# Extra matmuls of a constant tile ahead of each sub-layer's matmuls in a two-layer decoder trunk

## The reference

```python
x = x + 0.5 * rmsnorm(swiglu(rmsnorm(x, ng[0]), ffn1_in, ffn1_out), ng[1])
x = x + rmsnorm(mixer(rmsnorm(x, ng[2])), ng[3])
x = x + 0.5 * rmsnorm(swiglu(rmsnorm(x, ng[4]), ffn2_in, ffn2_out), ng[5])
```

## Time and profile before

| what | value |
|---|---|
| median of 3 runs | 2587.87 us (2587.82 to 2588.37) |
| span of the profiled execution | 2587.0 us |
| PE busy | 2483.4 us, 12094 records |
| DVE busy | 1368.0 us |
| ACT busy | 1032.3 us |
| POOL busy | 380.9 us |
| granted TensorE clock, mean | 0.982 |

### The profile page before, as it was taken

One profiled execution on the slowest core, in us unless ns is written; L12 is line 12 of the kernel. 1 busy time (PEld: TensorE's weight loads), 2 busy tenths in 40 slices (PEclk: granted clock), 3 DMA queues, 4 the chain that ended last, 5 costly groups with the idle time before them and its releaser, 6 DMA issues.

```text
span 2587.0 us, 34928 instructions
## 1 busy us (share of the span) xinstructions
PE 2483.4 (96%) x12094; PEld 2049.8 (79%) x12094; DVE 1368.0 (53%) x1874; ACT 1032.3 (40%) x1389; POOL 380.9 (15%) x276
## 2 busy tenths in 40 slices
PE   8999998998999999999999889999999889999997
PEld 7888876887788888788888678888888777788885
DVE  5445347665454443554433667666666642644533
ACT  5333335554443233433333445454455442432332
POOL 2111011000211110111101510000000001211100
PEclk9999999998999999999999989999999999999999
DMA  5332331221232233232233111111111102222232
GB/s 164 97 97 77 96 104 58 72 73 57 65 98 97 97 84 90 86 106 97 89 88 100 67 66 50 50 35 58 50 50 58 33 26 97 73 97 97 83 96 65
DMA packets 66912, 203.32 MB, mean 79 GB/s; under 512 B 7664, under 2 KB 11888, under 8 KB 66816
## 3 DMA queue, kind: packets, MB, share of 16 engines
q1 hardware_dynamic: 66816, 202.03, 24.7%
HBM read 199.87 MB, written 2.13 MB: 78 GB/s over the span
## 4 chain that ended last, share of the span: by engine, by line
PE 86%; DVE 6%; ACT 4%; issue 4%; DMA 0%; DVEq 0%; SPq 0%; ACTq 0%
PE bank L1282 68%; PE bank L1494 6%; PE bank L1487 5%; PE bank L1547 1%; ACT w_hi L448 1%; DVE resid L768 1%; PE bank L1576 1%; DVE gate L953 1%; DVE y L763 1%; DVE h_lo L753 1%; PE bank L1567 1%; PE bank L1586 1%; DVE neg_at L1029 0%; PE bank L1429 0%; DVE w_lo L749 0%
## 5 line engine op out<-in xcount | busy, mean ns | idle before, releaser
L749 DVE TENSOR_TENSOR w_lo<-raw,w_hi 128x1024 fp32r<-128x1024 f32 x405 | 581.8, 1454 | 490.6 <-ACT w_hi L448 490.6
L1282 PE MATMUL bank<-h_hi,w_hi 128*128 128x512 f32 x1784 | 712.1, 399 | 59.7 <-DVE h_lo L753 31.9
L1282 PE MATMUL bank<-h_hi,w_lo 128*128 128x512 f32 x1784 | 701.9, 393 | 0.0
L1282 PE MATMUL bank<-h_lo,w_hi 128*128 128x512 f32 x1720 | 676.7, 393 | 0.0
L448 ACT ACTIVATE w_hi<-raw 128x1024 fp32r<-128x1024 f32 x405 | 427.1, 1057 | 581.5 <-PE bank L1282 541.3
L1282 PEld LDWEIGHTS bank<-h_hi,w_hi 128*128 128x128 f32 x1784 | 339.9, 191 | 141.5 <-issue 40.2
L1282 PEld LDWEIGHTS bank<-h_hi,w_lo 128*128 128x128 f32 x1784 | 339.5, 190 | 72.5
L1282 PEld LDWEIGHTS bank<-h_lo,w_hi 128*128 128x128 f32 x1720 | 327.4, 190 | 69.7 <-issue 3.1
L1191 POOL TENSOR_TENSOR y<-y,up 128x512 f32<-128x512 f32 x88 | 174.2, 1979 | 743.1 <-DVE up L792 670.8
L1282 PE MATMUL bank<-act_hi,w_hi 128*128 128x512 f32 x704 | 278.1, 395 | 0.0
L1282 PE MATMUL bank<-act_hi,w_lo 128*128 128x512 f32 x704 | 278.1, 395 | 0.0
(11 more groups left out here) (238 smaller groups left out, 2822.4 us busy)
## 6 DMA issues: line engine op xcount, KB each, us to landing
raw<-in_ffn_in SPq DMA_DIRECT2D x172, 512.0 KB, 3.5
raw<-in_gd_in SPq DMA_DIRECT2D x49, 512.0 KB, 3.5
raw<-in_ffn_out SPq DMA_DIRECT2D x64, 384.0 KB, 3.1
raw<-in_ffn_out SPq DMA_DIRECT2D x64, 320.0 KB, 2.9
raw<-in_hg_in SPq DMA_DIRECT2D x32, 512.0 KB, 3.5
raw<-in_gd_out SPq DMA_DIRECT2D x16, 512.0 KB, 3.7
raw<-in_hg_out SPq DMA_DIRECT2D x8, 512.0 KB, 3.5
g_bc<-g_rows SPq DMA_DIRECT2D x8, 512.0 KB, 4.4
```

The source lines that it names most:

```text
L749: nc.vector.tensor_tensor(w_lo[:, r, :], raw[:, r, :], w_hi[:, r, :].bitcast(f32), ALU.subtract).then_inc(lo_split, 1)
L1282: ins = nc.tensor.matmul(dst, w, moving[ml][:, k, :], start=first and n == 0 and (wl, ml) == (0, 0), stop=last and n == len(ks) - 1 and wl ...
```

## The change

Ahead of everything else in head_start(s), PE issues 24 matmuls (sub-layer 0) or 19 matmuls (sub-layers 1 to 5) of ones x ones, 128 x 128 by 128 columns, plain fp32, into the first 128 columns of bank 7. Nobody reads the result. In sub-layer 0 PE first waits until ones is made; in the others there is no wait ahead of them. The wait for the weight units and for h_lo of the first chunk come behind them. In all 24 + 5 x 19 = 119 matmuls are added; nothing is removed.

```diff
+WARM = 19
+WARM_FIRST = 24
...
             def head_start(s):
 
                 u0 = first_unit[s]
+                if not s:
+                    pe.wait_ge(const_made, 1)
+                for _ in range(WARM if s else WARM_FIRST):
+                    nc.tensor.matmul(bank[7][:, 0:P], ones[:], ones[:], start=True, stop=True)
                 if s:
                     pe.wait_ge(lo_split, u0 + RING + SKEW)
                 for k in range(KD):
```

## The result

| | before | after |
|---|---|---|
| median, 6 runs each | 2588.41 us (2587.82 to 2589.22) | 2596.51 us (2595.87 to 2599.37) |
| span of the profiled execution | 2587.0 us | 2597.4 us |

The changed kernel is slower: ratio 1.0034, 95% interval 1.0023 to 1.0044; the medians lie 8.1 us apart. Forecast were 2584.8 us and a range of 2582.0 to 2588.0. The profiled execution of after is its slowest one, 2599.37, so the traces differ by 10.4 us where the medians differ by 8.1.

A forecast was written before the change was run, and what follows sets the result against it. PE was taken to bound the kernel, with 86% of the chain, though DVE paces the heads from chunk 5. Gains of 1.2 + 0.3 + 1.6 = 3.1 us off 2587.87 gave 2584.8, range 2582.0 to 2588.0.

The forecast's parts named there:

- cost nothing: Heads of sub-layers 1 to 5: 4.48 us of added matmuls lie wholly under ACT's and DVE's work, 0.3 us left.
- No DMA queue is touched: Whole change: the added matmuls affect no DMA queue, since SP waits for splits and not for PE; no cost booked.
- Sub-layer 0: Its head starts 1.4 us later, at 9.1, but runs at full speed: gain 1.2 us (0.9 to 1.8).
- DVE doesn't hold it: Sub-layer 0's head: h_lo of chunk 4 is there at 19.01, PE comes to it at 20.0, so no wait.
- Sub-layers 1 to 4: Heads: DVE sets the pace from chunk 5 on, so gains are only 0, 0.03, 0 and 0.3 us.
- Rival 1: Heads: every slow matmul saved is time saved, 13.1 us, for 2574.8; chance 0.05.
- the rule of the Trainium skill: Heads: advice against idle gaps between matmul bursts; by it the change is worth half of all six slow stretches.
- rival 2: Heads: the added matmuls don't hold or raise the clock; +6.7 us in all, 2594.6; chance 0.04.
- rival 3: Heads of sub-layers 1 to 5: clock unhelped but cost hidden; time within 1 us of 2587; chance 0.06.
- Sub-layer 5: Its head has a slow stretch of 4.80 us, like sub-layer 2's 4.97, so a gain of about 0.
- Later restarts: Slow stretches from 627 and 1496, drawn anew by the earlier start: gain 1.6 us, ends -1.0 and +3.5.
- The two mixers' time shifts by more than 4 us: Sign over the two mixers, named in advance as showing the prediction wrong; size over 4 us.

The follow-up runs named there:

- shift by 144: The kernel before plus 288 satisfied waits (144 instructions) in PE's idleness ahead of the DeltaNet loop, no matmul added; 2596.53 us, ratio 1.0034.
- shift by 130: The kernel before plus 260 satisfied waits (130 instructions) ahead of the DeltaNet loop; 2590.44 us in one run.
- experiments 1 to 6: Kernels made from before or after with satisfied waits or fewer added matmuls, moving the DeltaNet loop's start or end in the code; 2586.52 to 2598.18 us.
- experiment 2: The changed kernel plus 224 satisfied waits (112 instructions) ahead of the DeltaNet loop, two blocks of shift in all; 2587.84 us, ratio 1.0001.
- experiment 5: The changed kernel plus 108 instructions of satisfied waits inside the DeltaNet loop's body, moving its end but not its start; 2596.63 us in one run.
- experiment 6: The changed kernel with 16 instead of 24 added matmuls in sub-layer 0; 2586.52 us, ratio 0.9994.
- experiment 7: The changed kernel with 18 matmuls in sub-layer 0 and more such fillers in further PE idle times of HGRN2's last step and the DeltaNet; 2581.07 us, ratio 0.9971.
- shift by 160: The kernel before plus 320 satisfied waits (160 instructions) ahead of the DeltaNet loop; 2590.72 us in one run.
- experiment 4: For the 2587.87 us quoted: the changed kernel without its 24 matmuls in sub-layer 0, those of sub-layers 1 to 5 kept; ratio 1.0.

## Why the prediction was wrong

**What failed.** The section on the parts of the change counts 4.48 us of PE time under cover and finds that the added matmuls "cost nothing" in sub-layers 1 to 5. As time of PE that is right. What it never counts is that the 119 matmuls are also 476 instructions in PE's program, and that everything behind them moves. It has no term and no rival for that, and its sentence "No DMA queue is touched" is wrong: the queue that brings PE its instructions is one, with 65 loads instead of 61. So the harm was put at nothing, where it measured 8.1 us. The mechanism as the runs leave it: at each back edge of the DeltaNet loop the code is loaded anew, first the block that holds the loop's start and then, 3.0 to 3.1 us later (up to 3.6 in some kernels without a pause), the next. The wait for the first is always there, 4.2 to 5.1 us on the branch, and always covered by the 17 matmuls in PE's queue. With enough instructions between the start and the end of its block, PE is busy with them until the second load has come. After starts the loop two instructions ahead of the end of a block, and PE waits for the second load. The traces agree in all eight pauses of four kernels (after, the shifts by 144 and 130, the longer body): PE goes on 1.2 to 1.6 us behind the end of the second load (after: 1733.94 + 1.57 = 1735.51, and 1737.07; shift by 144: 1734.33 + 1.01 = 1735.34, and 1736.55; shift by 130: 1733.44 + 0.96 = 1734.40, and 1735.63). The pauses then lower the clock. At the first edge of after start to start is 4.73 instead of 0.33, and 14 matmuls at 0.42 instead of 0.23 add 2.7: 7.1 in all, the jump that the traces show. At the second it is 4.7.

How PE takes its code, why 1.2 to 1.6 us remain behind a load, and why the second load comes 3 us behind the first, no record shows. That the place of the loop's start decides is shown, by experiments 1 to 6. That the next load is what PE waits for rests on the times above, on the pauses at one and the same instruction at 130 and 144, and on the number of loads.

**Sub-layer 0: 1.2, measured 0.2.** The added matmuls ended near 8.6 and not at 9.1, within the bounds given. The step that failed is "DVE doesn't hold it": it checked one chunk against the old times of DVE. That chunk's h_lo came at 20.67 instead of 19.01, and the one before it was late too. PE is idle for 0.75 us by that, 1.1 from start to start. This place also differs from run to run. In nine profiled kernels without a filler at the start the sum stands between 28.8 and 30.9, mean 29.8, and in five with one between 28.4 and 29.9, mean 29.4. That is 0.4 us, which a spread of 1.5 to 2.1 us doesn't tell from nothing, and 16 of them (29.4) do no worse than 24.

**Sub-layers 1 to 4: right.** In sub-layers 1, 2, 3 and 4 gains of 0, 0.03, 0 and 0.3 were forecast, and 0.04, 0.05, 0 and 0.32 measured. The largest one, PE at the end of sub-layer 4's head in after, where before has 1463.37 and the kernel was 0.46 ahead by then:

```profile
1462.59 1.02 PE L1274 MATMUL bank<-acc,ones 128*128 128x512 f32 x2
```

PE meets DVE's chain earlier and waits for it. Rival 1, all slow matmuls saved, is out by this: the clock is 1.00 at the heads and the time isn't there. (It is this rival that the prediction's paragraph on the rule of the Trainium skill means, and not the second.) So are rivals 2 and 3, since the clock does hold.

**Sub-layer 5: 0, measured 0.6 lost.** PE waits 0.97 us twice there; one addition on DVE (L770, at 2224.41) took 1.81 us instead of 0.69. It isn't the change: in the five other kernels with the same 19 matmuls there (experiments 2, 5, 6, 7 and the one without the first 24) the distance to before stays the same over this head within 0.02 us.

**Later restarts: 1.6, measured 0.** The slow stretch behind 627 is as long as before, and so is that behind 1484. Of this term's bounds, -1.0 and +3.5, neither was reached. These stretches do differ from kernel to kernel: from 627 to 688 the shift by 160, without an added matmul, gained 0.7 us on before, experiment 2 gained 0.7, and the kernel of experiment 5 lost 0.2. So what was booked as a gain of the change is a spread that other kernels show without it.

**Without the shift** the forecast's mechanism gives what experiments 2, 4 and 6 measured, 2587.84, 2587.87 and 2586.52: within the range. Part of that is luck: none of the three can be told from before's 2588.0, and the 1.6 us booked for later restarts is no effect of the change. It was the range that rested on too few kinds of harm. "The two mixers' time shifts by more than 4 us" was named as what would show the prediction wrong, and that is how it showed.

## What to carry to other kernels

Instructions have a place as well as a duration: where a loop is so long that its code is loaded anew in every iteration, any edit ahead of the loop can move its start to just before the end of a block, and here that cost 8 us, more than the 3.1 that the edit was forecast to gain. When an edit that should be neutral loses a few us, compare the timelines at the loops' back edges and look at the instruction queue; a few waits that are satisfied at once, put into an idle stretch, tell it apart from the edit's own effect, and can mend it. And keep the clock up only where PE leads the chain afterwards: the same fillers gave 0 to 0.3 us at heads that DVE paces and 5.2 us in a step that ends on PE.

## What the runs showed of the hardware

- The same loop, with the same body, passes its back edge with 0 to 0.8 us of idleness or with 3.0 to 4.3, by where it starts. The bad zone is narrow: of eleven distances from the old place, counted in blocks of 256, one had the full stall (144, in three kernels, by fillers or by waits) and one, 130, a partial one, while 115 and 160 had none. Both pauses sit 146 instructions behind the old start.
- The taken branch of that loop keeps PE's sequencer for 4.2 to 5.1 us in every kernel, and 17 queued matmuls cover it.
- At the first edge the second instruction load took 1.57 us in after and 1.01 in the shift by 144; the pause was 4.33 against 3.07 us, so the load's own time makes up 0.6 of the 1.3 us between them.
- An instruction of two waits that are satisfied at once costs PE 0.11 us once nothing covers it.
- Products of a constant tile of ones, 128 columns wide, count as work for the clock: it stayed at 1.00 through 4.4 us of nothing else, at the heads of sub-layers 1, 4 and 5 in after.
- The releaser named at such a stall is only the instruction on another engine that happened to end last: a w_lo that the matmul doesn't need, 0.54 us ahead of it.
